# A hybrid diffusion step in fp32: the conditioning products of the merge and output stages move from TensorE to VectorE

## What is computed

```python
cond  = [c_ctx, c]                                   # two vectors of 2048: context, latent
mods  = silu(cond) @ w_ada + b_ada                   # 2048 x 12288: (shift, scale, gate) x 2
h     = rms_norm(x) * (1 + scale1) + shift1
...
merged = sum_i sigmoid(h @ w_gate_i) * (branch_i @ w_i_out)   # i = ssd, attention, pool
x     = x + gate1 * (merged @ w_out)
x     = x + gate2 * moe(rms_norm(x) * (1 + scale2) + shift2)
```

## Time and profile before

| | |
|---|---|
| median of three runs | 2671.36 us (2671.11 to 2679.62) |
| the profiled execution | 2671.49 us, its span 2669.7 us |
| TensorE matmul busy | 2281.4 us, 85% of the span |
| VectorE busy | 1525.7 us, 57% |
| ScalarE busy | 1126.7 us, 42% |
| L347 and L348, matmuls of conditioning tiles | 256 each, 104.3 and 101.0 us busy |
| L156, low parts | 832, 1004.9 us, 1223 ns each |
| granted TensorE clock, mean | 0.915 of full |

### The profile page before, as it was taken

The page is one execution under the profiler, slowest core; times in us unless marked ns, Lnnn a source line. Parts: engine busy times, 40 slices in busy tenths (PEclk is TensorE's granted clock), DMA queues, the critical chain, the costliest instruction groups (busy, mean ns, idle before and its releaser), DMA issues. The chain is left out here.

```text
span 2669.7 us, 29102 instructions
## 1 busy us (share of the span) xinstructions
PE 2281.4 (85%) x11340; PEld 1939.8 (73%) x11340; DVE 1525.7 (57%) x2064; ACT 1126.7 (42%) x1445; POOL 8.4 (0%) x12
## 2 busy tenths in 40 slices
PE   5869945699998888999979997996699999999994
PEld 3569934589997345989959896885677777777772
DVE  4857457444432543454344544545477988879884
ACT  4833322333333133333323333333256766667671
POOL 0000000000000000000000000000000000000000
PEclk9979955799999577999989998998799999999996
DMA  6923311255532002545424454552068988889881
GB/s 226 374 73 128 120 58 48 91 173 181 172 132 95 4 0 74 171 169 179 134 87 169 171 178 164 200 179 95 19 235 277 341 286 318 313 286 342 285 296 50
DMA packets 126856, 459.94 MB, mean 172 GB/s; under 512 B 15408, under 2 KB 17232, under 8 KB 126320
## 3 DMA queue, kind: packets, MB, share of 16 engines
q1 hardware_dynamic: 126704, 457.92, 49.4%
HBM read 453.88 MB, written 3.98 MB: 172 GB/s over the span
## 5 line engine op out<-in xcount | busy, mean ns | idle before, releaser
L156 DVE TENSOR_TENSOR wlo<-raw,whi 128x1024 fp32r<-128x1024 f32 x832 | 1004.9, 1223 | 663.7 <-ACT whi L150 650.4
L150 ACT ACTIVATE whi<-raw 128x1024 fp32r<-128x1024 f32 x832 | 870.1, 1058 | 917.3 <-PE bank L168 629.5
L166 PE MATMUL bank<-hhi,whi 128*128 128x384 f32 x1664 | 561.9, 338 | 55.1 <-DVEq L1353 17.6
L168 PE MATMUL bank<-hhi,wlo 128*128 128x384 f32 x1664 | 557.2, 335 | 0.0
L167 PE MATMUL bank<-hlo,whi 128*128 128x384 f32 x1664 | 557.1, 335 | 0.0
L166 PEld LDWEIGHTS bank<-hhi,whi 128*128 128x128 f32 x1664 | 313.3, 188 | 77.5 <-issue 59.6
L167 PEld LDWEIGHTS bank<-hlo,whi 128*128 128x128 f32 x1664 | 313.4, 188 | 0.0
L168 PEld LDWEIGHTS bank<-hhi,wlo 128*128 128x128 f32 x1664 | 313.2, 188 | 0.0
L1828 PE MATMUL bank<-whi,group_hi 128*128 128x512 f32 x512 | 203.1, 397 | 4.3 <-DVE wlo L156 3.1
L1830 PE MATMUL bank<-wlo,group_hi 128*128 128x512 f32 x512 | 201.3, 393 | 0.0
L1829 PE MATMUL bank<-whi,group_lo 128*128 128x512 f32 x512 | 200.5, 392 | 0.0
(11 more groups left out here) (324 smaller groups left out, 2660.4 us busy)
## 6 DMA issues: line engine op xcount, KB each, us to landing
raw<-in_dense SPq DMA_DIRECT2D x448, 512.0 KB, 3.9
raw<-in_moe SPq DMA_DIRECT2D x384, 512.0 KB, 4.9
cs_rows_bc<-cs_rows SPq DMA_DIRECT2D x8, 768.0 KB, 3.9
x_mix<-in_x SPq DMA_DIRECT2D x1, 3072.0 KB, 15.4
merged<-in_x SPq DMA_DIRECT2D x4, 768.0 KB, 6.4
out_y<-merged SPq DMA_DIRECT2D x4, 768.0 KB, 3.3
pool_w_sb<-in_pool_w SPq DMA_DIRECT2D x1, 1024.0 KB, 6.2
w_router_sb<-in_w_router SPq DMA_DIRECT2D x1, 1024.0 KB, 4.7
```

The costliest lines, as they stand in the source:

```text
L150: self.nc.scalar.activation(self.whi[:, n % W, :], self.raw[:, n % R, :], ACT.Copy).then_inc(self.hi_done, 1)
L156: self.nc.vector.tensor_tensor(self.wlo[:, n % W, :], self.raw[:, n % R, :], self.whi[:, n % W, :].bitcast(F32), ALU.subtract).then_inc(se ...
L166: self.nc.tensor.matmul(out, self.whi[:, s, c], xhi[:, k, :], start=(k == 0), stop=False)
L168: last = self.nc.tensor.matmul(out, self.wlo[:, s, c], xhi[:, k, :], start=False, stop=(k == blocks - 1))
```

## The change

A conditioning tile of the merge and output stages no longer goes through ScalarE and TensorE. VectorE multiplies the raw fp32 tile with the per-partition columns of silu(cond) and sums into an accumulator of 128 x 512 for each of the two conditionings: two row blocks times two conditionings, four operations a tile (`ada_tile`). When the chunk's eight tiles are done, TensorE sums the accumulators over partitions with eight matmuls against one column of ones (`ada_sums`), and VectorE adds the bias (`ada_add`). The order of the tiles, LEAD, R and W are unchanged. The buffers `whi` and `wlo` and their semaphores count own tiles alone (`own`), and a load that follows a conditioning tile waits for that tile's products. `ada_settle_phase` is gone: silu(cond) and `b_ada` lie from the start where they can stay. `norm_phase` takes its semaphores from a shared pair and counts on.

```diff
     def load(self, sp, n):
         if n >= R:
-            sp.wait_ge(self.lo_done, n - R + 1)
+            if self.is_ada(n - R):
+                sp.wait_ge(self.ada_ops, 4 * (n - R - self.own(n - R)) + 4)
+            else:
+                sp.wait_ge(self.lo_done, self.own(n - R) + 1)
...
     def act_hi(self, act, i, body, t):
         n = self.tile(i, body, t) + LEAD
+        if self.is_ada(n):
+            return
+        j = self.own(n)
         act.wait_ge(self.landed[n % R], 16 * (n // R + 1))
-        if n >= W:
-            act.wait_ge(self.used, n - W + 1)
+        if j >= W:
+            act.wait_ge(self.used, j - W + 1)
...
     def dve_lo(self, dve, i, body, t):
         n = self.tile(i, body, t) + LEAD
-        dve.wait_ge(self.hi_done, n + 1)
+        if self.is_ada(n):
+            self.ada_tile(dve, n)
+            return
+        j = self.own(n)
+        dve.wait_ge(self.hi_done, j + 1)
...
+    def ada_tile(self, dve, n):
+        a = n - self.own(n)
+        chunk, u = a // ADA_BODY, a % ADA_BODY
+        dve.wait_ge(self.landed[n % R], 16 * (n // R + 1))
+        if u == 0 and chunk >= 2:
+            dve.wait_ge(self.ada_summed, chunk - 1)
+        for kk in range(2):
+            for g in range(2):
+                op, k = 4 * a + 2 * kk + g, 2 * u + kk
+                acc = self.ada_acc[:, chunk % 2, g, :]
+                w, c = self.raw[:, n % R, kk * 512:kk * 512 + 512], self.csilu[:, k, g:g + 1]
+                if k == 0:
+                    self.nc.vector.tensor_scalar(acc, w, c, None, ALU.mult).then_inc(self.ada_ops, 1)
+                else:
+                    dve.wait_ge(self.ada_ops, op - 1)
+                    self.nc.vector.scalar_tensor_tensor(out=acc, in0=w, scalar=c, in1=acc, op0=ALU.mult, op1=ALU.add)\
+                        .then_inc(self.ada_ops, 1)
+
+    def ada_sums(self, pe, chunk):
+        pe.wait_ge(self.ada_ops, 4 * ADA_BODY * (chunk + 1))
+        if chunk:
+            pe.wait_ge(self.ada_added, chunk)
+        for q in range(4):
+            for g in range(2):
+                last = self.nc.tensor.matmul(self.bank[6][:, 2 * q + g:2 * q + g + 1],
+                                             self.ada_acc[:, chunk % 2, g, q * P:q * P + P], self.ones[:, 0:1],
+                                             start=True, stop=True)
+        last.then_inc(self.ada_summed, 1)
+
+    def ada_add(self, dve, chunk):
+        cols = slice(4 * (ADA_FIRST + chunk), 4 * (ADA_FIRST + chunk) + 4)
+        dve.wait_ge(self.ada_summed, chunk + 1)
+        self.nc.vector.tensor_tensor(self.mods[:, cols, :], self.bank[6][:, 0:8].rearrange("p (q g) -> p q g", q=4),
+                                     self.b_ada[:, cols].unsqueeze(2).to_broadcast([P, 4, 2]), ALU.add)\
+            .then_inc(self.ada_added, 1)
...
 def merge_phase(N, ohi, olo, first, name):
...
-                    if t == ada_end + 1:
-                        ada_row(N, act, i, body, ada_end)
-                ada_turned(N, act, i)
...
-                ada_add(N, dve, st, i)
+                N.ada_add(dve, N.ada_chunk + i)
...
                     if kind == "ada":
-                        ada_product(N, pe, i, body, t, o)
                         continue
...
                     if t == body - 1:
-                        ada_transposes(N, pe, i)
+                        N.ada_sums(pe, N.ada_chunk + i)
```

More of the change, by code:

```diff
@@ L89, in __init__ @@
         self.hlo = sb("hlo", [P, KB, T], F32R)
+        self.csilu = sb("cond_silu", [P, KB, 2], F32)
+        self.b_ada = sb("b_ada_sb", [P, 96], F32)
         self.merged_at = self.at
@@ L103, in __init__ @@
         self.dense_tiles, self.moe_tiles = io.dense.shape[0] - R, io.moe.shape[0] - R
+        self.ada_ops, self.ada_summed, self.ada_added = [self.sem("ada_" + n) for n in ("products", "summed", "added")]
+        merge, w_out = [kind for kind, _ in MERGE_ORDER] * 4, [kind for kind, _ in OUT_ORDER] * 4
+        self.kinds = ["own"] * (ADA_FIRST * ADA_BODY + 2 * SSD_BLOCKS) + merge + ["own"] * (2 * ATT_BLOCKS) + merge \
+            + ["own"] * (2 * POOL_BLOCKS) + merge + w_out
+        assert len(self.kinds) == self.dense_tiles
+        self.own_before = [0]
+        for kind in self.kinds:
+            self.own_before.append(self.own_before[-1] + (kind == "own"))
     def keep(self, name, shape, dt):
@@ L127, in tile, with own, is_ada @@
         return i * body + self.tile0 + t
+    def own(self, n):
+        return self.own_before[n] if n <= self.dense_tiles else self.own_before[-1] + n - self.dense_tiles
+    def is_ada(self, n):
+        return n < self.dense_tiles and self.kinds[n] == "ada"
     def load(self, sp, n):
         if n >= R:
-            sp.wait_ge(self.lo_done, n - R + 1)
+            if self.is_ada(n - R):
+                sp.wait_ge(self.ada_ops, 4 * (n - R - self.own(n - R)) + 4)
+            else:
+                sp.wait_ge(self.lo_done, self.own(n - R) + 1)
         src = self.io.dense[n] if n < self.dense_tiles else self.io.moe[(n - self.dense_tiles) % self.moe_tiles]
@@ L163, in pe_tile @@
-        pe.wait_ge(self.lo_done, n + 1)
+        s = self.own(n) % W
+        pe.wait_ge(self.lo_done, self.own(n) + 1)
         for kk in range(8):
@@ L171, in tiles_done @@
     def tiles_done(self, i, body, t):
-        return self.tile(i, body, t) + 1
+        return self.own(self.tile(i, body, t) + 1)
 def ada_phase(N):
@@ L194, in ada_phase @@
     consts_in, x_in = sem("consts_in"), sem("x_in")
-    s_sq, s_sqsum, s_row, s_tr, s_four, s_add = [
-        sem("ada_" + n) for n in ("squares", "sqsum", "row", "tr", "four", "add")]
-    N.ada_sems, N.ada0 = (s_row, s_tr, s_four, s_add), chunks
+    s_row, s_tr, s_four, s_add = [sem("ada_" + n) for n in ("row", "tr", "four", "add")]
+    s_sq, s_sqsum = N.squares_ready, N.squares_summed = sem("squares_ready"), sem("squares_summed")
+    N.norm_done = 4
+    N.ada_chunk = 0
     with nc.Block() as block:
@@ L336 @@
 OUT_ORDER = among(8, "oo" "aaa" "oo" "aaa" "oo" "aa" "oo")
[L339 to L384, removed]
 def modulate_phase(N, part, gain, name):
@@ L876, in _ @@
                                        op0=ALU.mult, op1=ALU.subtract).then_inc(s_olo, 1)
[L879 to L893, removed]
 def merge_phase(N, ohi, olo, first, name):
@@ L1390, in norm_phase @@
     sq = N.keep("squares_" + name, [P, 2, 4, T], F32)
-    s_sq, s_sum = [N.sem(name + n) for n in ("_squares", "_sums")]
+    s_sq, s_sum, done = N.squares_ready, N.squares_summed, N.norm_done
     with nc.Block() as block:
@@ L1396, in _ @@
                 if b >= 2:
-                    act.wait_ge(s_sum, b - 1)
+                    act.wait_ge(s_sum, done + b - 1)
                 nc.scalar.activation(sq[:, b % 2], xt[:, 4 * b:4 * b + 4, :], ACT.Square).then_inc(s_sq, 1)
@@ L1402, in _ @@
             for b in range(4):
-                pe.wait_ge(s_sq, b + 1)
+                pe.wait_ge(s_sq, done + b + 1)
                 for k in range(4):
@@ L1411, in _ @@
             st = N.steps(dve)
-            dve.wait_ge(s_sum, 4)
+            dve.wait_ge(s_sum, done + 4)
             st.chain(nc.vector.tensor_scalar(N.rs_v[:, :], N.bank[7][:, 0:T], 1.0 / D, EPS, ALU.mult, ALU.add))
             rsqrt_steps(dve, nc, st, N.rs_v[:, :], N.rstd[:, :], N.rs_t[:, :])
+    N.norm_done += 4
 def rank_steps(st, nc, v, ahead, after, before, rank):
@@ L1822, in product @@
                 def product(i, t, out, parts, k0, first, last):
-                    s = N.tile(i, body, t) % W
-                    pe.wait_ge(N.lo_done, N.tile(i, body, t) + 1)
+                    s = N.own(N.tile(i, body, t)) % W
+                    pe.wait_ge(N.lo_done, N.own(N.tile(i, body, t)) + 1)
                     for kk in range(2):
```

20 lines of the change are left out of this document (8 added, 12 removed).

## The result

The changed kernel takes 2810.85 us (median of four runs, 2808.77 to 2811.89), 1.051 times the kernel before (interval 1.049 to 1.053). It is slower by 136 us: the kernel before, run beside it, took 2674.44 us (median of four). The forecast was 2772 us, 100 us slower, in a range of 2705 to 2812. The profiled execution's span is 2808.9 us against 2669.7, 139 us more.

The account below looks back on a forecast made before the run. TensorE's stream was taken to bound the merge and output stages. Longer waits, sums and the removed phase gave +42 us, clock falls +58, together +100 on 2671.5: 2772 us, range 2705 to 2812 (own range 2750 to 2802).

Parts of the forecast that it names:

- What bounds the stages, and where the third tile stands: Merge and output stages: TensorE's stream sets the end; the third tile's products come behind the wait for the own tile.
- the chain evacuation, third tile, low part: VectorE's order behind a group of three: next own matmul +0.94 us in first merge, +1.54 attention and pool, +1.04 output.
- Price of a product: VectorE, 128x512 product on a conditioning tile: 0.668 us each, bounds 0.64 and 0.78; 2.67 us a tile.
- The sums: End of each body: eight one-column matmuls replace four transposes, 0.9 us against 0.37, +0.53 each, 8.5 us in all.
- The clock: Merge and output stages: TensorE's clock falls in each of 32 stops, 1.8 us lost each, +58 us, between 42 and 80.
- dear case: Rival: products cost 0.78 us, groups of two also drop the clock, 2.5 us lost a stop; up to 2822 us; chance 0.08.
- The phase that moved constants: Before the first merge: the phase goes, so the merge starts earlier, -2.3 us, bounds 0 and -2.7.
- The clock holds: Rival, merge and output stages: clock never falls, 2714 us, or in half the stops, 2743; chance 0.17 (holds or few falls).
- Faster: the third tile hidden: Rival: third tile's products and next low part done before the own tile ends, about 2510 us; chance 0.04.

Follow-up runs that it names:

- the even order: Only the two order lists changed, conditioning tiles singly between own tiles: changed kernel 2543.72 us (0.9525 of before); kernel before with the same lists 2672.78 us (0.9994).
- the kernel with the low part ahead: Changed kernel with a group's third conditioning tile and the next own tile's low part ahead of VectorE's wait for the own tile: 2556.49 us, 0.956 of before.

## Why the prediction was right, and what was sized wrong

The direction and the mechanism were right. That the time lies inside the range is in part luck: 2810.85 is above the forecast's own range (2750 to 2802) and 1 us below the end of the stated one (2812), and the sum was 100 us where 136 to 139 were measured. Two terms were too small, the clock by 29 us and the sums by 13.

- **What bounds the stages, and where the third tile stands.** Right, and this carried the sign. The rows of before gave the chain evacuation, third tile, low part; after shows it within 0.04 us for every kind of group, and moving one tile in VectorE's order took 84 us out of the waits.
- **Price of a product.** 0.668 us forecast from L871 and L1758, 0.66 measured (2.66 for four, 746 ns for one). The lower of the two values, for a wait on the one before the last, was right. The Trainium skill, "VectorE: DVE Perf Modes", section "The DRAIN you can't avoid", has the next operation start only when the pipe is empty, but adds that one which is not held starts earlier; the prediction left out that addition. The trace agrees with the addition: 0.66 from start to start is less than the 0.746 of one, and the 10 us more that the prediction worked out by the rule didn't come. The 0.594 us that it held beside its own price was too low.
- **The sums.** This term was mis-sized: +8.5 against +21.4 us. The step that failed is "six such with four columns in 0.81 us": those six records come from three matmuls of the code, since an fp32 matmul stands twice in the trace. After has 16 records for eight sums. I took a price per record and multiplied it with a count of the code. The upper bound, 1.08 us, had the same fault, and no rival held the 13 us.
- **The clock.** The mechanism was right (the filled stops show it, 86 us), the size was not: 58 against 87. Both factors were low. I counted 32 falls, and there were 42 more than before: the stops of 2.7 us, which the earlier trace rows seemed to spare with 2.8, fell in all 8 cases, and two of 2.0 us did. And a fall behind a long stop cost 4.8 us of work at the lower level in the mean, not 3.9: 2.2 us lost where 1.8 was forecast. The "dear case" of the rivals named both of these, the falls behind the 2.7 us stops and the dearer fall (2.5 us there). A single stop of 2.8 us that was spared carried that step; of 73 stops of 2.7 to 3.1 us in the table above two were spared. The earlier trace rows had a sign of it: the mean of 0.85 over the 3.30 us without matmuls is 1.0 us at 0.50, so the clock fell some 2.3 us into that stop, and not only "after 3.3 us".
- **The phase that moved constants.** -3.5 us; 2.2 lie in the wait before the first merge (17.5 to 15.3, and 15.3 in the experiments too). The other 1.3 were there ahead of it and are no effect of the change that can be told: the first merge starts at 496.9 to 502.9 us in the profiles of kernels that are the same up to there.
- **The rivals.** "The clock holds" fell. "Faster: the third tile hidden" named the right point of decision and its price: forecast 2510 if it were so, and with the order changed 2556 and 2544. What it left out is the 13 us of the sums, and the output stage, where products in a bunch (or, in the even order, short waits) still hold up a low part.

## What to carry to other kernels

Work that moves from the busy engine to one with room helps only if it does not stand, in that engine's queue, between an evacuation and the operand that the busy engine waits for: read who releases the bound engine, and list what is queued between. A stop of TensorE costs more than its length: behind nearly every stop of 2.7 us or more here some 3.4 to 5 us of matmuls ran at half the clock. So the 48 stops of the changed kernel made it 35 us longer than before by themselves and 87 by the clock, and shortening the long ones by 1.1 us returned only that length. Compare the records of an operation with the count in the code before multiplying.

## What the runs showed of the hardware

- **Short stops are not safe.** Behind groups of conditioning tiles, 25 of 52 stops of 1.9 to 2.1 us were followed by a fall, and 183 of 185 of 2.7 us and more. The fall can come after the restart, as at 1125.9 above, so that it doesn't look like the stop's doing.
- **Filling the stops pays.** 24 useless matmuls in each long stop and 10 in each short one held the clock at 1.00 and made the kernel 80 us faster. The own tile behind them started as far behind its S as without them (4.94 us in the first merge).
- **A stage that nothing touches can move.** The attention stage between two merges has frequent short waits, and its clock goes up and down. The same 404 records took 189.0 us (clock 0.67) to 201.4 us (0.60) in the profiles of this study. By stretches, of the kernel before:

```profile
849.90:1042.90 193.00, 157.05 (x404) 72.24 (x403) 80.30 (x262) 53.12 (x166) 0.00 (x0) 0.65 0.02 7
```

and of the kernel with the low part ahead:

```profile
808.70:1010.10 201.40, 168.37 (x404) 76.47 (x402) 80.25 (x262) 53.07 (x166) 0.00 (x0) 0.60 0.02 6
```

That is 8 us between these two from one stage with not a line of it changed, which is as much as 0.3% of the kernel. What sets the clock's course in it from run to run is not settled here.
